# A two-layer encoder step on one core: the second attention's projections move between scores and turn, with a third probability buffer

## What is computed

```python
def diff_attention(q, k, v, q_pos, k_pos, ...):          # 6 heads, two maps m each, dim 64
    logits = jnp.einsum('bqhmd,bkhmd->bhmqk', qb, k) * scale
    logits = logits + bias                               # relative position, per head
    probs = masked_softmax(logits, chunk_mask(qp, k_pos))
    attn = probs[:, :, 0] - lam * probs[:, :, 1]
    return jnp.einsum('bhqk,bkhe->bqhe', attn, v)        # then rmsnorm

def memory_attention(q, mem_k, mem_v):                   # 4 heads, dim 64, 256 memory rows
    probs = softmax(q . mem_k * scale);  return probs . mem_v
```

## Time and profile before

| what | value |
|---|---|
| median of 3 runs | 949.15 us (947.65 to 956.57) |
| the profiled execution's own time | 951.2 us |
| its span, first to last instruction | 949.4 us |
| TensorE busy | 796.8 us (84% of the span) |
| VectorE busy | 331.0 us (35%) |
| ScalarE busy | 185.2 us (20%) |
| moved by DMA | 273.30 MB, mean 288 GB/s |

### The profile page before, as it was taken

How to read it: one execution, slowest core, us unless ns; L and a number is a source line. 1 busy time by engine, 2 the same in 40 slices (tenths; PEclk the granted TensorE clock), 3 DMA queues, 4 the chain that set the end, 5 groups by cost and what they waited for, 6 DMA issues and landing times.

```text
span 949.4 us, 9961 instructions
## 1 busy us (share of the span) xinstructions
PE 796.8 (84%) x3956; PEld 395.7 (42%) x3956; DVE 331.0 (35%) x729; ACT 185.2 (20%) x450; POOL 44.0 (5%) x58
## 2 busy tenths in 40 slices
PE   6998999989999978777899788979899997877650
PEld 3665777453433322222444566655444332222210
DVE  1034454453422322113540353463453331212128
ACT  1213333010311211110110144511013111101010
POOL 1021000002000000000200000000110000000010
PEclk9998999997999999999999997989899999999885
DMA  9633008656999999999694600580789999999943
GB/s 361 213 107 145 1 1 320 256 241 224 401 429 424 426 425 428 424 427 409 201 405 130 252 2 1 212 364 21 300 328 421 428 426 425 424 427 424 422 138 102
DMA packets 43872, 273.30 MB, mean 288 GB/s; under 512 B 6424, under 2 KB 11230, under 8 KB 26160
## 3 DMA queue, kind: packets, MB, share of 16 engines
q1 hardware_dynamic: 32032, 243.66, 62.3%
q0 software_dynamic: 5888, 19.95, 6.3%
q10 hardware_dynamic: 5904, 9.04, 2.7%
HBM read 253.88 MB, written 18.73 MB: 287 GB/s over the span
## 4 chain that ended last, share of the span: by engine, by line
PE 53%; DMA 25%; DVE 11%; SPq 6%; ACT 2%; issue 2%; ACTq 0%; POOL 0%; DVEq 0%; POOLq 0%
DMA arena<-in_expert_w_up 23%; PE bank L889 16%; PE bank L831 6%; PE bank L903 5%; PE bank L1123 4%; PE bank L818 3%; SPq L476 2%; PE bank L754 2%; PE bank L806 2%; PE bank L912 2%; PE bank L799 1%; DVE arena L1831 1%; PE bank L651 1%; PE bank L732 1%; DMA arena<-expert_rows,out_row 1%
## 5 line engine op out<-in xcount | busy, mean ns | idle before, releaser
L889 PE MATMUL bank<-arena 128*64 128x512 f32 x1024 | 240.3, 626 | 49.8 <-DMA arena<-in_expert_w_up 48.1
L889 PEld LDWEIGHTS bank<-arena 128*64 128x64 f32 x1024 | 77.1, 144 | 209.8 <-issue 147.9
L903 PE MATMUL bank<-arena 128*64 128x512 f32 x512 | 116.9, 598 | 16.6 <-DVE arena L1753 16.6
L1753 DVE COPY arena<-bank 128x256 f32<-128x256 f32 x32 | 13.6, 424 | 280.1 <-PE bank L896 280.1
L903 PEld LDWEIGHTS bank<-arena 128*64 128x64 f32 x512 | 33.9, 136 | 77.5 <-issue 54.8
L1317 ACT ACTIVATE arena<-bank 128x256 f32<-128x256 f32 x32 | 12.3, 383 | 267.1 <-PE bank L889 267.1
L1761 DVE RECIPROCAL arena<-arena 128x256 f32<-128x256 f32 x32 | 56.1, 1753 | 1.1
L831 PE MATMUL bank<-arena 128*128 128x512 f32 x128 | 56.0, 595 | 0.0
L1123 PE MATMUL bank<-arena 128*128 128x512 f32 x96 | 41.7, 594 | 3.6 <-DVE arena L1454 3.6
L818 PE MATMUL bank<-arena 128*128 128x288 f32 x128 | 37.9, 456 | 4.1 <-DVE arena L1860 4.1
L1339 ACT COPY arena<-bank 128x512 f32<-128x512 f32 x32 | 18.8, 586 | 98.7 <-PE bank L903 98.7
(11 more groups left out here) (250 smaller groups left out, 869.7 us busy)
## 6 DMA issues: line engine op xcount, KB each, us to landing
arena<-in_expert_w_gate SPq DMA_DIRECT2D x32, 2048.0 KB, 21.1
arena<-in_expert_w_up SPq DMA_DIRECT2D x32, 2048.0 KB, 26.2
arena<-in_expert_w_down SPq DMA_DIRECT2D x64, 1024.0 KB, 28.6
arena<-in_w_out SPq DMA_DIRECT2D x4, 2048.0 KB, 9.5
expert_rows<-arena ACTq DMA_DIRECT2D x64, 128.0 KB, 7.8
arena<-in_w_kv_shared SPq DMA_DIRECT2D x3, 2048.0 KB, 9.3
arena<-in_w_mem_kv SPq DMA_DIRECT2D x2, 2048.0 KB, 20.1
arena<-sorted_rows POOLq DMA_DIRECT2D x2, 2048.0 KB, 9.1
```

What stands on the lines that cost most here:

```text
L889: last = mm(bank[j][64 * half:64 * half + 64, :].rearrange("p (u f) -> p u f", u=2), slots[:, k, 0:CAP], w[:, :, k, 256 * half:256 * half ...
L903: last = mm(bank[3 + j][64 * n:64 * n + 64, :], hid_t[:, j, c, 64 * half:64 * half + 64], w[:, half, c, 512 * n:512 * n + 512], start=(hal ...
```

## The change

TensorE, ScalarE and VectorE all take the jobs of step n + 1 behind the scores, exponentials and statistics of step n, and the jobs of step 0 ahead of the loop. ScalarE's `exps` of step n stand ahead of `turned` of step n - 2. The probabilities get three buffers instead of two; they lie in slot 5, down slot 1, so expert 1's down weights are now issued behind its gate and up weights. The job `kvs` gets bank 5 for itself, so the attention starts without waiting until it is emptied; the steps that use bank 5 or the sample keys wait instead.

```diff
-        prob1 = zb.cut(2, 2, 384)
+        prob1 = arena[:, 5 * SLOT:5 * SLOT + 3 * 768].rearrange("p (j m k) -> p j m k", j=3, m=2)
...
-                job_bank.append(6 + n % 2 if name in diff_jobs else RING0 + n % RING)
+                job_bank.append(6 + n % 2 if name in diff_jobs else RING0 if name == "kvs" else RING0 + n % RING)
...
                 load_down(l, 0, 0, dn_in[0])
-                load_down(l, 1, 1, dn_in[1])
+                if l == 0:
+                    load_down(0, 1, 1, dn_in[1])
                 sp.wait_ge(o_ready, sum(NS[:l + 1]))
                 load_up(l, 1, ups[1], up_in[1])
+                if l == 1:
+                    load_down(1, 1, 1, dn_in[1])
...
                     elif kind == "dp":
-                        if h == 0:
+                        if h == 1:
                             pe.wait_ge(*emptied(max(i for i in range(job0["qd0"]) if job_bank[i] == 5)))
...
+                if l == 1:
+                    for name in beside[0]:
+                        queries_keys(name)
                 for n in range(NS[l] + O_LAG):
                     if l == 0 and n < NS[0] and n >= 5 and (n - 5) % 5 == 0:
                         keys_queries((n - 5) // 5)
-                    if l == 1:
-                        for name in beside.get(n, ()):
-                            queries_keys(name)
                     if n < NS[l]:
                         scores(n)
+                    if l == 1:
+                        for name in beside.get(n + 1, ()):
+                            queries_keys(name)
                     if 0 <= n - T_LAG < NS[l]:
                         turn(n - T_LAG)
...
                 if name == "kts":
+                    pe.wait_ge(*emptied(job0["kvs"]))
...
-            for n in (job0["kvs1"] + 1, job0["kvs"]):
+            for n in (job0["kvs1"] + 1, job0["kvs1"] + 2):
                 pe.wait_ge(*emptied(n))
             attention(1)
...
-                    if s0 + n >= 2:
-                        ac.wait_ge(pt_ready, s0 + n - 1)
+                    if s0 + n >= 2 + l:
+                        ac.wait_ge(pt_ready, s0 + n - 1 - l)
...
+                if l == 1:
+                    new_queries(0)
                 for n in range(NS[l] + O_LAG):
...
-                    if l == 1:
-                        for name in beside.get(n, ()):
-                            for k, b in jobs(name):
-                                dst = qd_feat if name[1] == "d" else qm1_feat
-                                out_of(nc.scalar.mul(dst[:, int(name[2]), :], b[:, 0:NT], BD ** -0.5))
+                    if l == 1 and n < NS[l]:
+                        exps(n)
+                        new_queries(n + 1)
                     if 0 <= n - T_LAG < NS[l]:
                         turned(n - T_LAG)
-                    if n < NS[l]:
+                    if l == 0 and n < NS[l]:
                         exps(n)
...
                     elif kind == "dp":
-                        if s0 + n >= 2:
-                            ve.wait_ge(pt_ready, s0 + n - 1)
+                        ve.wait_ge(pt_ready, s0 + n - 2)
...
+                else:
+                    new_keys(0)
                 for n in range(NS[l] + O_LAG):
...
                     if n < NS[l]:
                         stats(n)
                     if 1 <= n <= NS[l]:
                         post(n - 1)
+                    if l == 1:
+                        new_keys(n + 1)
                     if n >= O_LAG:
                         outputs(n - O_LAG)
```

More of the change, by code:

```diff
@@ L727, in turn @@
                         pe.wait_ge(pt_copied, s0 + n)
-                    p = prob[:, n % 2, :] if l == 0 else prob1[:, n % 2].rearrange("p a b -> p (a b)")
+                    p = prob[:, n % 2, :] if l == 0 else prob1[:, n % 3].rearrange("p a b -> p (a b)")
                     b = bank[2]
@@ L1244, in exps @@
                                 c = 2 * i + m
-                                last = f(prob1[:, n % 2, m, a:z], prob1[:, n % 2, m, a:z], ACT.Exp,
+                                last = f(prob1[:, n % 3, m, a:z], prob1[:, n % 3, m, a:z], ACT.Exp,
                                          bias=neg_max[:, n % 3, c:c + 1], accum_out=row_sum[:, n % 3, c:c + 1])
@@ L1279, in squares, with new_queries @@
                               accum_out=head_ss[0:rows, t, hd:hd + 1]))
+                def new_queries(n):
+                    for name in beside.get(n, ()):
+                        for k, b in jobs(name):
+                            dst = qd_feat if name[1] == "d" else qm1_feat
+                            out_of(nc.scalar.mul(dst[:, int(name[2]), :], b[:, 0:NT], BD ** -0.5))
+                if l == 1:
+                    new_queries(0)
                 for n in range(NS[l] + O_LAG):
@@ L1554, in stats @@
                     elif kind == "dp":
-                        if s0 + n >= 2:
-                            ve.wait_ge(pt_ready, s0 + n - 1)
+                        ve.wait_ge(pt_ready, s0 + n - 2)
                         for m in range(2):
-                            own(tt(prob1[:, n % 2, m, :], s_bank(l, n, m)[:, 0:384], bias_p[:, h, :], ALU.add))
+                            own(tt(prob1[:, n % 3, m, :], s_bank(l, n, m)[:, 0:384], bias_p[:, h, :], ALU.add))
                         own.settle()
                         for i, (a, z) in enumerate(SEGS[kind]):
-                            own(red(nm[:, 2 * i:2 * i + 2], prob1[:, n % 2, :, a:z], AX.X, ALU.max, negate=True),
+                            own(red(nm[:, 2 * i:2 * i + 2], prob1[:, n % 3, :, a:z], AX.X, ALU.max, negate=True),
                                 stats_ready if i else None)
                     elif kind == "ds":
-                        if s0 + n >= 2:
-                            ve.wait_ge(pt_ready, s0 + n - 1)
-                        p = prob1[:, n % 2].rearrange("p a b -> p (a b)")[:, 0:NSK]
+                        ve.wait_ge(pt_ready, s0 + n - 2)
+                        p = prob1[:, n % 3].rearrange("p a b -> p (a b)")[:, 0:NSK]
                         step(tt(p, b[:, 0:NSK], bias_s[:, h, :], ALU.add))
@@ L1588, in post @@
                         for i, (a, z) in enumerate(SEGS[kind]):
-                            own(stt(prob1[:, n % 2, 0, a:z], prob1[:, n % 2, 1, a:z], ri[:, 2 * i + 1:2 * i + 2],
-                                    prob1[:, n % 2, 0, a:z], ALU.mult, ALU.add), probs_ready if i else None)
+                            own(stt(prob1[:, n % 3, 0, a:z], prob1[:, n % 3, 1, a:z], ri[:, 2 * i + 1:2 * i + 2],
+                                    prob1[:, n % 3, 0, a:z], ALU.mult, ALU.add), probs_ready if i else None)
                         return
@@ L1616, in outputs, with new_keys @@
                                 o_copied if j == 3 else None)
+                def new_keys(n):
+                    for name in beside.get(n, ()):
+                        for k, b in jobs(name):
+                            if name == "kts":
+                                out_of(V.tensor_copy(kd_feat[:, :, 512:NK],
+                                                     b[:, 0:BH * DEC].rearrange("p (h n) -> p h n", n=DEC)))
+                            else:
+                                out_of(V.tensor_copy(kd_feat[:, int(name[2]), 0:512], b[:, :]))
                 if l == 0:
                     ve.wait_ge(out_mem, 32)
+                else:
+                    new_keys(0)
                 for n in range(NS[l] + O_LAG):
@@ L1625, in attention @@
                         keys_queries((n - 5) // 5)
[L1626 to L1633, removed]
                     if n < NS[l]:
```

## The result

The changed kernel took 940.74 us (median of 6 runs, 933.6 to 945.19); the kernel before, run beside it, 949.23 (median of 6, 946.92 to 956.57). The ratio on record is 0.9863, with a 95% interval from 0.9822 to 0.9904: faster by 1.4%. It isn't the quotient of the two medians, which is 0.991. A second set of runs, later, gave 934.53 against 954.82, ratio 0.9819 [0.9769, 0.9869]. The forecast was 938.0, a ratio of 938.0 / 949.15 = 0.988. One slow run, of 942.81 us in the last table of the experiments, is left out of its median.

What follows compares the result with a forecast made beforehand. Bound: a chain of TensorE, VectorE and ScalarE taking turns in the attention, later waits for expert weights. Savings of 14.6 us less 3.4 for the clock give 11.2, so 938.0 us against the 949.15 median; range 932.5 to 946.0.

Steps and rivals of the forecast that it cites:

- The start: Sample job in the fifth bank: first dp scores of the second attention begin at 533.9 instead of 538.64, saving 4.7 us.
- The waits: Second attention: projections and keys between scores and turn cover TensorE's waits, saving 2.6, 1.1 and 0.4 us.
- The clock: Two later slow spots of TensorE in the second attention: 5.8 us recovered if the clock stays up.
- The fall charged with 3.4 us: Clock falls again behind the two waits at the sample scores, slowing values, scores and projection: 3.4 us, bounds 0 and 4.3.
- Third buffer: Three probability buffers: statistics wait for the turn three back, already done, so a cost of nothing.
- Moved DMAs: Expert 1's last two down weights issued behind its up weights, almost 100 us before first use: nothing.
- the rival in which the gain stops short of the end: DMA paces the last third; if the stream can't start earlier, time stays 949.2; chance 0.09, wholly or in part.
- ScalarE's queue: Rival: the copy of turned probabilities behind each exponential group makes dp steps wait; 10 us slower, 959.3; chance 0.06.
- The other clock rival: Clock comes back in none of three places in the attention: 6.6 us charged, 8.0 left, 941.2; chance 0.22.
- The absolute numbers I named: First dp scores at about 533.9, attention's last output copy near 608.5, SyncE's issue of expert 3's weights near 686.7.

Runs made afterwards that it cites:

- the presets moved: The changed kernel with VectorE's presets (bias mask, sample rows of the mixed output, norm sums) ahead of the sample job's copies instead of behind them; 936.85 us.

## Why the prediction was right, and where it was off

The whole attention from dp0's scores on takes the sum apart: busy time shows the clock, the rest the waits. The kernel before, and the bank alone in its timed set (whose clock was full); the changed kernel's row, 536.63 to 606.70, stands above:

```profile
538.64:619.90 81.26, 70.36 (x435) 50.58 (x435) 35.73 (x99) 38.44 (x147) 0.82 (x2) 0.92 0.26 102
```

```profile
534.58:609.80 75.22, 64.31 (x435) 46.15 (x435) 35.69 (x99) 38.75 (x147) 0.83 (x2) 1.00 0.35 134
```

- **The start, 4.7 us forecast: exact.** dp0's scores began 6.57 us after the sample job (539.95 - 533.38), 11.27 before: 4.70. VectorE was late by the presets, and the wait was the 2 us named.
- **The waits, 2.6 + 1.1 + 0.4 = 4.1 forecast: about 4.35.** Those ahead of dp3 to dp5 and the turn's 1.07 are gone; the memory scores' is 0.27 instead of 0.63; at the sample scores 1.08 and 1.11 (forecast 1.2 and 1.1) replace 1.61 and 0.67. All waits behind dp0 add up to 9.7 us before and 5.4 after.
- **The clock, 5.8 us at most: 70.36 - 64.31 = 6.05** of TensorE's time, at equal work and equal waits. The size held, the reason did not: I had tied the two later slow spots to the waits ahead of them, but the bank alone, in its timed set, kept all these waits (9.7 us in sum) and got the 6.05 us back. The order and buffers without the bank had no later slow spot either. So taking those waits away was not needed for it, and as far as the reason goes this term came right by luck. The order takes another 0.7 off its busy time (64.31 to 63.63), which no term had. 4.7 + 4.35 + 6.05 + 0.7 = 15.8 = 92.40 - 76.58, where I had 14.6.
- **The fall charged with 3.4 us: the size held, 3.23; the reason did not.** It came in the first profile just where I put it, values, scores and a projection of 5.54 us. But the step that the pair "resembles the pair of 1.61 and 0.67 us after which the clock fell, so I take it to fall again" read more into the waits than they say. Of three profiles of the changed kernel, with waits equal to 0.01 us, one had the fall; the bank alone, in its timed set, kept 1.61 and 0.67 and no projection was slow. With the presets moved, the fall came again (5.72 us); without the bank it did not. A term with a chance, one in three or two in five by these few profiles, is what the runs support.
- **Third buffer: right only together.** "A cost of nothing" held; the sentence that without it the moved turn would hold the statistics is what 99.81 us of stretch showed.
- **Moved DMAs, nothing: right.** The tail is 329.41 against 329.63, and expert 3's issue is early by the stretch's gain; the rival in which the gain stops short of the end is out.
- **ScalarE's queue: refuted, with its sign reversed.** No dp scores waited on it. The Trainium skill, "TensorE: Matmul & The Clock Gate", section "Architectural detail: the array is 16x 32x32, not 1x 128x128", has ScalarE work strictly in queue order. The rows agree (the 4.51 us behind L1292), but the order that this rule punishes here is the copy first. The rival's turning point was also worked out wrongly: 0.6 us to spare over four hops is 0.15 us a hop, the cost read there, and not 0.3. By that sum it stood nearer than I said.
- **The other clock rival** (a fall in all three places, 941.2) came nearest to the first median by its number, and by none of its rows: one slow place was seen, or none.

The absolute numbers I named (533.9, 608.5, 686.7) were missed by 6.1, 4.7 and 4.6 us in the first profile, because it reached the stretch 6.0 us late; counted from the sample job's end they are met to 1.5 us. The median of 940.74 is 2.7 us over the forecast and 934.53 is 3.5 under it: both inside what the stream ahead of the stretch and one clock fall move. The same holds for the medians' gains, 8.5 and 20.3 us, where the stretch gained 12.6 and 15.8; no profile of before was kept from the timed set, so there it isn't shown where the rest lies.

What stays open: why the kernel before lost the clock at the same three places in both of its profiles, while the bank alone, with the same later waits, lost almost nothing in two, and the order and buffers alone lost it at the first place only. The runs are too few to say that the bank or the order itself keeps it.

## What to carry to other kernels

Put the next step's projection between a step's scores and its turn, so that the copies out of the banks hide behind products; but count the buffers, since the moved turn frees its buffer later, and keep exponentials ahead of the copy that waits for that turn. A job that is emptied late gets a bank of its own. Where executions differ upstream, measure the changed stretch between two landmarks, and see that the tail keeps its length.

## What the runs showed of the hardware

Unchanged code upstream took a different time from one execution to the next: the sample job ended between 521.85 and 535.10 us in the 14 profiles. The expert products of layer 0 took some 222 us in six of them and 224.4 to 226.0 in the others, with nothing between. And the granted clock does not follow from the waits alone that the profile shows: it was 0.65 and 1.00 at the same place, behind the same 1.08 and 1.11 us.
